# Attention as one staged pipeline that also projects its gates, and eight output-gate tiles computed beside the rwkv inputs

## The reference

```python
def attention_mixer(u_lat, u_ctx, ...):       # 8 query heads, 2 key/value heads, head size 128
    q, k, v, z = jnp.split(u @ w_in, ...)
    q = rms_norm(q, q_norm_g); k = rms_norm(k, k_norm_g)      # per head
    ql = apply_axial_rope(ql, ...); kl = apply_axial_rope(kl, ...)
    y = softmax(ql @ concat(kc, kl).T * d ** -0.5) @ concat(vc, vl)
    return (y * silu(z)) @ w_out
...
    p = rmsnorm(x, norm1_w) @ w_in
    z, xbc, dt_raw, p_rwkv, p_hgrn, p_gate = jnp.split(p, in_splits, axis=-1)
    y_ssm = ssd_branch(...)   @ w_branch_ssm      # ends with rmsnorm(y, ssm_norm_w)
    y_rwkv = rwkv7_branch(p_rwkv, ...) @ w_branch_rwkv
    y_hgrn = hgrn2_branch(p_hgrn, ...) @ w_branch_hgrn
    gates = jax.nn.sigmoid(p_gate).reshape(b, L, 3, 1024)
    mixed = gates[:, :, 0] * y_ssm + gates[:, :, 1] * y_rwkv + gates[:, :, 2] * y_hgrn
    x = x + mixed @ w_out
```

## Time and profile before

| | us |
|---|---|
| median of 3 runs | 2381.48 |
| lowest and highest run | 2377.84, 2381.9 |
| profiled execution, its own time | 2380.35 |
| its span in the trace | 2378.6 |

### The profile page before, as it was taken

The page is one execution under the profiler, slowest core; times in us unless marked ns, Lnnn a source line. Parts: engine busy times, 40 slices in busy tenths (PEclk is TensorE's granted clock), DMA queues, the critical chain, the costliest instruction groups (busy, mean ns, idle before and its releaser), DMA issues. The chain is left out here.

```text
span 2378.6 us, 40862 instructions
## 1 busy us (share of the span) xinstructions
PE 2021.5 (85%) x16732; PEld 1484.7 (62%) x16732; DVE 1059.6 (45%) x2136; ACT 577.9 (24%) x1248; POOL 76.0 (3%) x51
## 2 busy tenths in 40 slices
PE   5889898998989898896955687867989999879997
PEld 2356666565666656345633576644776798768886
DVE  4345756656575665102134318776445433211101
ACT  2033443434344343002012103222332321000000
POOL 0000110101010010000000000000000000000000
PEclk9889998999999998897967888986999999989998
DMA  8610101011010100212300132111012222324443
GB/s 332 266 54 2 55 1 56 1 55 55 2 55 1 55 1 2 106 71 76 107 0 0 71 118 107 71 66 41 29 55 94 82 101 85 110 106 156 162 159 124
DMA packets 50339, 183.72 MB, mean 77 GB/s; under 512 B 5744, under 2 KB 7152, under 8 KB 49648
## 3 DMA queue, kind: packets, MB, share of 16 engines
q1 hardware_dynamic: 50160, 181.18, 20.6%
HBM read 180.11 MB, written 1.05 MB: 76 GB/s over the span
## 5 line engine op out<-in xcount | busy, mean ns | idle before, releaser
L826 PE MATMUL banks<-u,w_ring 128*128 128x512 f32 x768 | 357.0, 602 | 6.6 <-PEq L195 6.6
L406 PE MATMUL banks<-u,w_ring 128*128 128x256 f32 x1088 | 248.4, 390 | 13.5 <-PEq L195 13.5
L406 PEld LDWEIGHTS banks<-u,w_ring 128*128 128x128 f32 x1088 | 212.4, 197 | 47.2 <-issue 17.8
L826 PEld LDWEIGHTS banks<-u,w_ring 128*128 128x128 f32 x768 | 141.7, 193 | 137.6 <-issue 134.5
L485 PE MATMUL banks<-u,w_ring 128*128 128x256 f32 (+1 forms) x640 | 158.7, 412 | 17.2 <-PEq L195 17.2
L485 PEld LDWEIGHTS banks<-u,w_ring 128*128 128x128 f32 x640 | 125.7, 197 | 49.9 <-issue 33.6
L485 PE MATMUL banks<-gated,w_ring 128*128 128x512 f32 (+1 forms) x384 | 141.0, 530 | 3.0 <-PEq L195 3.0
L485 PEld LDWEIGHTS banks<-gated,w_ring 128*128 128x128 f32 x384 | 74.0, 193 | 69.6 <-issue 66.3
L424 ACT ACTIVATE sq<-h 128x256 f32<-128x256 f32 (+1 forms) x40 | 14.5, 444 | 349.7 <-PEq L195 349.7
L853 DVE SCALAR_TENSOR_TENSOR acc<-raw,hc,acc 128x512 f32<-128x512 f32 x128 | 96.2, 752 | 4.6
L382 PE MATMUL banks<-u,w_ring 128*128 128x256 f32 x384 | 88.2, 380 | 0.0
(11 more groups left out here) (468 smaller groups left out, 3248.8 us busy)
## 6 DMA issues: line engine op xcount, KB each, us to landing
w_ring<-in_w SPq DMA_DIRECT2D x323, 512.0 KB, 6.0
h<-in_h SPq DMA_DIRECT2D x2, 2048.0 KB, 9.5
const_base<-in_const SPq DMA_DIRECT2D x1, 1216.0 KB, 5.4
const_part<-in_const SPq DMA_DIRECT2D x1, 1024.0 KB, 4.9
out<-u SPq DMA_DIRECT2D x1, 1024.0 KB, 4.8
const_part<-in_const SPq DMA_DIRECT2D x1, 640.0 KB, 4.4
const_part<-in_const SPq DMA_DIRECT2D x1, 512.0 KB, 3.5
w_rows<-in_rows SPq DMA_DIRECT2D x1, 512.0 KB, 5.7
```

The source lines that it names most:

```text
L406: last = nc.tensor.matmul(out, lhs[k], rhs[k], start=(k == 0), stop=(k == n - 1))
L826: mm = nc.tensor.matmul(self.places[m % len(self.places)][:, :], st.slot(m)[:, P * k:P * k + P], u[:, k, :], start=(k == 0), stop=(k == KT ...
```

## The change

Five things change together.

1. Attention is one stage, `attention`. The keys' part and the four pairs of heads stand in one set of lists. The softmax of a pair, its transposes and its value products run beside the scores of the next pair and the normalisation of the one after.
2. The eight gate tiles of attention are no longer projected ahead. Their 64 products stand in the new stage, between its first steps. The weight stream is reordered to key and value, query, gate.
3. Two of 24 output-gate tiles take the place of the padding in `ssd_heads`, and six more (48 products) are projected in `rwkv_inputs`. Since their place (`early`, the latent half of `h`) is still needed, `h` is stored to DRAM (`hold`, 1 MB) after norm1 and loaded back after the first `gated_linear`.
4. The norm of `ys` and its barrier are gone as a stage; its squares, adds, root and scaling stand in `rwkv_inputs`. There the small loads are waited for by the engines that need them.
5. `hgrn_heads` has 16 gate tiles left, four products in each level.

```diff
+def attention(nc, st, bank, C, pqz, pkv, qg, kg, rope, kf, v_t, gated, src):
...
+    extra = BesideGroups(nc, st, src, pqz[:, ATT_Q:2 * ATT_Q, :], ATT_Q, [bank[6][:, 0:SEQ], bank[5][:, 0:SEQ]], s, 0)
+    extra.per_group = 4
+    st.in_stage(ATT_Q // 4, 4, s["x_summed"], block)
...
+        def query_sums(i):
+            pe.wait_ge(s["q_sq"], i + 1)
+            pe.wait_ge(s["q_ready"], i)
+            column_sums(nc, C, bank[7], qsq[:, i % 2, :], 4).then_inc(s["sums"], 1)
...
+        def scores(i, n):
+            if n == 0:
+                pe.wait_ge(s["q_ready"], i + 1)
+            if i == 0 and n == 0:
+                pe.wait_ge(s["k_ready"], ATT_KV)
+            if i:
+                pe.wait_ge(s["exped"], 4 * i + n - 3)
+            nc.tensor.matmul(bank[n][:, :], tile(q_of(i), n), kf[:, i // 2, :], start=True, stop=True).then_inc(s["scores"], 1)
+        def turn(i, n):
+            at = 4 * i + n
+            pe.wait_ge(s["probs"], at + 1)
+            if at >= 2:
+                pe.wait_ge(s["turned_out"], at - 1)
+            else:
+                pe.wait_ge(s["x_out"], ATT_Q)
+            for t in range(TT):
+                mm = nc.tensor.transpose(tile(bank[4 + n % 2], t), tile(pr[:, i % 2, n, :], t), C("ident"))
+            mm.then_inc(s["turned"], 1)
+        def outs(i, j):
+            pe.wait_ge(s["turned_out"], 4 * i + 2 * j + 2)
+            if i and j == 0:
+                pe.wait_ge(s["gated"], i)
+            accumulate(nc, bank[6][:, SEQ * j:SEQ * j + SEQ], [v_t[:, i // 2, t, :] for t in range(TT)],
+                       [pt[:, j, t, :] for t in range(TT)]).then_inc(s["out"], 1)
...
+        extra.products(pe, 4)
+        pe.wait_ge(s["k_sq"], ATT_KV)
+        column_sums(nc, C, bank[7], ksq, ATT_KV * TT)
+        pe.wait_ge(s["q_sq"], 1)
+        column_sums(nc, C, bank[7][:, ATT_KV * TT:], qsq[:, 0, :], 4).then_inc(s["sums"], 1)
+        pe.wait_ge(s["v_out"], ATT_KV)
+        extra.products(pe, 12)
+        pe.wait_ge(s["root"], 1)
+        for h in range(ATT_KV + 1):
+            spread(nc, C, bank[h], rc[:, TT * h:TT * h + TT], TT).then_inc(s["spread"], 1)
+        extra.products(pe, 6)
+        for h in range(ATT_KV):
+            pe.wait_ge(s["k_norm"], h + 1)
+            nc.tensor.matmul(bank[3][:, SEQ * h:SEQ * h + SEQ], C("rot"), kf[:, h, CTX:TOK], start=True,
+                             stop=True).then_inc(s["k_rot"], 1)
+        query_turn(0)
+        query_sums(1)
+        extra.products(pe, 18)
+        query_roots(1)
+        for n in range(4):
+            scores(0, n)
+        extra.products(pe, 8)
+        query_turn(1)
+        extra.products(pe, 16)
+        for i in range(pairs):
             for n in range(4):
+                turn(i, n)
+                if i + 1 < pairs:
+                    scores(i + 1, n)
+                if i and n == 0:
+                    outs(i - 1, 1)
+                if i + 2 < pairs and n == 0:
+                    query_sums(i + 2)
+                if i + 2 < pairs and n == 1:
+                    query_roots(i + 2)
+                if i + 2 < pairs and n == 3:
+                    query_turn(i + 2)
+            outs(i, 0)
+        outs(pairs - 1, 1)
...
+        squared(1)
+        for c in range(5):
+            extra.copy_tile(act, link)
+        for n in range(4):
+            exped(0, n)
+            if n:
+                extra.copy_tile(act, link)
+        squared(2)
+        for i in range(pairs):
             for n in range(4):
+                turned(i, n)
+                if i + 1 < pairs:
+                    exped(i + 1, n)
+                if n == 2:
+                    gate(i)
+                if i + 3 < pairs and n == 3:
+                    squared(i + 3)
...
+        for i in range(pairs):
             for n in range(4):
+                if i + 1 < pairs:
+                    negmax(i + 1, n)
+                at = 4 * i + n + 2
+                if at < 4 * pairs:
+                    probs(at // 4, at % 4)
+                if i + 2 < pairs and n == 0:
+                    mean(i + 2)
+                if i + 2 < pairs and n == 2:
+                    scaled(i + 2)
+                if i + 2 < pairs and n == 3:
+                    roped(i + 2)
+                if i and n == 1:
+                    finished(i - 1)
+        finished(pairs - 1)
...
+def rwkv_inputs(nc, st, bank, C, src, ys, norm_cols, early, spilled, loaded, p, ps, tmp, mu0, mu1, w_up, g_up, a_up, vecs, w0_rows, lw, g_t, aa, kk, rc, bonus):
...
+        extra = BesideGroups(nc, st, src, early[:, 2:8, :], 6, [bank[b][:, 0:SEQ] for b in (6, 7, 6, 7, 4, 5)], s, 0, half_tanh=True)
+        extra.per_group = 6
+        st.in_stage(1, 6, s["x_summed"], block)
...
+            extra.products(pe, 2 * KT)
+            pe.wait_ge(*loaded)
...
-            pe.wait_ge(s["gd"], 1)
-            for t in range(ST):
-                nc.tensor.matmul(bank[6 + t][:, :], ps[:, 13, P * t:P * t + P], g_up[:, :], start=True, stop=True).then_inc(s["g_raw"], 1)
+            pe.wait_ge(s["x_out"], 1)
+            extra.products(pe, KT)
...
+            pe.wait_ge(s["x_out"], 3)
+            pe.wait_ge(s["n_added"], KT - 1)
+            column_sums(nc, C, bank[6], sq[:, 0, :], ST).then_inc(s["n_summed"], 1)
+            extra.products(pe, KT)
+            pe.wait_ge(s["a_in"], 4)
+            extra.products(pe, KT)
...
+            pe.wait_ge(s["n_root"], 1)
+            spread(nc, C, bank[6], roots, ST).then_inc(s["n_spread"], 1)
+            pe.wait_ge(s["gd"], 1)
+            for t in range(ST):
+                pe.wait_ge(s["x_out"], 4 + t)
+                nc.tensor.matmul(bank[(7, 4)[t]][:, :], ps[:, 13, P * t:P * t + P], g_up[:, :], start=True,
+                                 stop=True).then_inc(s["g_raw"], 1)
+            extra.products(pe, KT)
...
+            act.wait_ge(spilled, 16)
+            extra.copy_tile(act, link)
+            extra.copy_tile(act, link)
+            link(nc.scalar.activation(early[:, 0:2, :], p[:, n:n + 2, :], ACT.Tanh, scale=0.5))
+            for k_in in range(KT):
+                nc.scalar.activation(sq[:, k_in, :], ys[:, k_in, :], ACT.Square).then_inc(s["n_squared"], 1)
+            act.wait_ge(s["kk_raw"], 1)
+            link(nc.scalar.activation(tmp[:, 0:4, :], kk, ACT.Square), s["kk_sq"])
...
+            for k_in in range(1, KT):
+                dve.wait_ge(s["n_squared"], k_in + 1)
+                link(nc.vector.tensor_tensor(sq[:, 0, :], sq[:, 0, :], sq[:, k_in, :], ALU.add), s["n_added"])
+            dve.wait_ge(s["kk_sum"], 1)
+            link(nc.vector.tensor_scalar(rc[:, 0:16], bank[0][:, 0:16], 1e-12, None, ALU.add), s["mean"])
...
+            dve.wait_ge(s["n_summed"], 1)
+            link(nc.vector.tensor_scalar(roots, bank[6][:, 0:ST], 1.0 / D, EPS, ALU.mult, ALU.add), s["n_mean"])
...
+            dve.wait_ge(s["n_spread"], 1)
+            for k_in in range(KT):
+                link(nc.vector.scalar_tensor_tensor(ys[:, k_in, :], ys[:, k_in, :], norm_cols[:, k_in:k_in + 1], bank[6][:, 0:SEQ],
+                                                    ALU.mult, ALU.mult))
...
-                project(nc, st, bank, 4, 4, lambda k: u[:, k, CTX:TOK], SEQ, pqz)
                 project(nc, st, bank, 1, 4, lambda k: u[:, k, :], TOK, pkv)
+                project(nc, st, bank, 2, 4, lambda k: u[:, k, CTX:TOK], SEQ, pqz)
                 finish_loads(nc, loads, small)
-                with ExitStack() as e3:
-                    sq = sb("sq1", [P, 2 * TOK], e3)
-                    rs = sb("rs1", [P, TOK], e3)
-                    attention_keys(nc, bank, C, pkv, cc("kg"), rope, kf, v_t, sq, rs)
-                attention_heads(nc, bank, C, pqz, cc("qg"), rope, kf, v_t, gated)
+                attention(nc, st, bank, C, pqz, pkv, cc("qg"), cc("kg"), rope, kf, v_t, gated, lambda k: u[:, k, CTX:TOK])
...
+        hold = nc.dram_tensor("hold", (P, KT, SEQ), F32).ap()
+        early = h[:, :, CTX:TOK]
+        start_loads(nc, [(hold, early)], late)
...
-                norm(u, u, cc("ssm_norm_w"), 0)
-                finish_loads(nc, loads, small)
-                rwkv_inputs(nc, bank, C2, p_rw, ps, tmp, cc("rwkv_mu", 0, 14), cc("rwkv_mu", 14, 28), up[0:64], g_up, a_up,
+                rwkv_inputs(nc, st, bank, C2, latent, u[:, :, 0:SEQ], cc("ssm_norm_w"), early, late, (small, loads), p_rw, ps, tmp, cc("rwkv_mu", 0, 14), cc("rwkv_mu", 14, 28), up[0:64], g_up, a_up,
...
-                hgrn_heads(nc, st, bank, banks, C2, cs, p_hg, lf, kf, cc("hgrn_norm_w"), yh, work, latent, gates, 24, 6)
+                hgrn_heads(nc, st, bank, banks, C2, cs, p_hg, lf, kf, cc("hgrn_norm_w"), yh, work, latent, gates[:, 8:24, :], 16, 4)
...
-                gated_linear(nc, st, bank, count, 4, src, tiles, gates[:, 8 * b:8 * b + 8, :])
+                own = gates[:, 8 * b:8 * b + 8, :]
+                gated_linear(nc, st, bank, count, 4, src, tiles, own if b else early, own)
+                if b == 0:
```

(19 more changed lines are left out.)

261 lines of the change are left out of this document (127 added, 134 removed).

## The result

The changed kernel takes 2294.22 us (median of 4 runs, 2291.12 to 2297.01), the kernel before 2381.38 in the same session; the ratio is 0.9637, interval 0.9620 to 0.9653. That is 87 us less; the forecast was 2288 and 94 less.

A forecast was written before the change was run, and what follows sets the result against it. TensorE alone bounds hgrn; in attention no engine is full and work goes from hand to hand. From 2380.35 us, -27.6 - 32 - 27 - 8 + 0.5 = -94.1 gives 2286.2, stated as 2288; range 2276 to 2300, 8 in 10 2273 to 2308.

The forecast's parts named there:

- Projection, -27.6: Projection ahead of attention: 8 of 16 tiles of 256 leave it at 3.45 us each, 27.6 us less.
- Attention's stage, 92 forecast: Merged attention stage: 78 us of TensorE work plus 13 of waits, end at 92 against 124, 32 less.
- the detour of the roots: Attention loop: root of the pair after next goes over VectorE and GpSimd; 2 us in each of two pairs, 1 in third.
- The bounds of 79 and 141: Attention stage: 79 us with no wait at all, 141 with no overlap of pairs.
- hgrn, -27: hgrn stage: two of six products leave each of 32 levels, level 4.38 to 3.52 us; 27 less, bounds 22 and 28.
- Norm and rwkv inputs, -8: Norm merged into rwkv inputs: end at 1631.7 against 1639.9, 8 us less; bounds 12 less and 0.
- Store and load of `h`, +0.5: 1 MB store ahead of the weights at 1367 and its load back: 0.5 us more, bounds 0 and 4.
- Rival 1: Attention loop's steps lock together: a pair takes 15.3 us, loop 12 to 20 longer, total 2300 to 2308; chance 0.14.
- Rival 2: The rwkv merge gives nothing, as products sit ahead of what VectorE waits for: total 2296; chance 0.07.
- Rival 3: Clock stays low in the attention loop, 36 us of TensorE work double at worst: +35, total 2323; chance 0.06.
- the 2322: Total in us if the attention loop ran at about 1.2 GHz by the skill's clock rule.
- Rival 4: Fuller TensorE is given 1.2 GHz; in hgrn 127 us become 254, total 2415, slower than before; chance 0.02.

The follow-up runs named there:

- the second time: The changed kernel run again, unchanged, on the last experiment's chip: 2293.82 us (5 runs, 2291.68 to 2294.90).
- experiment 5: Changed kernel with all sixteen gate tiles projected ahead again and no gate products in attention, pairs still overlapped: 2304.41 us, 0.9684 of the kernel before.
- Experiment 7: Changed kernel with one of eight products of each gate tile in the rwkv inputs and hgrn stages, waits, copies and loads kept: 2246.33 us, 0.9439.
- six other executions: The changed kernel's second run and five experiments' runs with the same rwkv inputs lists, one without the wait for the store; that stage with its gap: 49.6 to 49.8 us.
- Experiments 3 and 10: 3: changed kernel, rwkv inputs' barrier before the small loads, 2293.52 us. 10: barrier, small loads, then weights, plus two attention reorderings, 2285.04 us.
- experiment 8: Changed kernel without the store of half of `h` to HBM, its reload and the waits for them: 2294.69 us, 0.9638 of the kernel before.
- after: The changed kernel itself, with all five parts of the change: 2294.22 us, 0.9637 of the kernel before.
- experiment 4: Changed kernel with ten of attention's eighteen gate products moved behind the second pair's query sums, eight left ahead: 2289.40 us, 0.9614 of the kernel before.

## Why the prediction held, and where it was off

- **Projection, -27.6:** measured to 0.1 us. The price of a tile (3.45 us) came from a stage that TensorE filled before and after.
- **Attention's stage, 92 forecast:** 95.3 and, the second time, 93.7. Its waits, put at 13, are 13.6 (TensorE is busy for 81.7 of the 95.3), but in other places. The uncovered wait for the second pair's sums was 3.56 (forecast 3.4). The five us that I gave to the detour of the roots were one wait of 0.97; in its place TensorE waits for the scaled and rotated query (1.24, 2.26 and twice 0.52). What was mis-sized is the work, 81.7 for 78: the sum was at full clock, and the stage's first half was granted 0.93. Twelve products from 1168.66 and eighteen from 1185.94 took 6.9 and 9.4 us, where 0.432 each gives 5.2 and 7.8; that is 3.3 of the 3.7. The bounds of 79 and 141 were needlessly wide, but experiment 5 shows the order of things: the merge with its overlap 47 us, filling about 10.
- **hgrn, -27:** -29.1. The level came out to 0.01 us. The 0.6 I held back for the heads' borders did not appear, and the stage's start ran warmer (3.9 us from its first matmul to the first level's sums, 4.8 before), as did its end by 0.3; neither was forecast. Experiment 7 says why it was safe: TensorE stays the bound there with seven eighths of its products gone, so little else could come late.
- **Norm and rwkv inputs, -8:** -4.2, and -2.7 to -2.9 in six other executions: the step that failed. Two terms were wrong. The wait for the norm's spread, put at 3, was 4.56, and 5.8 to 6.0 in the six others: the sixteen products ahead of it were reckoned at full clock (6.9 us) and took 8.5 and 9.8 to 10.0. So the stage proper is 44.3 us from the barrier, and 45.6 to 45.8 in the others, 7.5 to 6.0 less than 51.8 and not 8. What I left out altogether is the opening: the five loads are now issued in front of the barrier, and each engine stands 4.0 us for SyncE, where 0.7 lay between the stages before. I had counted a moved step's instructions on the compute engines and not its loads on SyncE's queue. Experiments 3 and 10 show that this is the queue and not the data: with the barrier issued first the gap is 1.2 us, and the 2.8 us reach the stage's end.
- **Store and load of `h`, +0.5:** nothing in the stages beside them (experiment 8).
- **Rival 1** (steps lock): the first three pairs began their transposes 11.8 and 14.4 us apart (1211.22, 1222.99, 1237.43), not 15.3, and the difference of the two is a values product (1.7), which the first interval doesn't hold, and longer waits for the query, less the wait for the root. **Rival 2** (the merge gives nothing): gave 6.0 to 7.5 inside the stage. **Rival 3** (clock low in the loop): 1.00 in the loop. My reading of busy share against clock was wrong both ways: the loop, busy for 81%, had 1.00 where I put 0.93, and the first half, busy for 43.64 of 48 us, had 0.93 where I put full clock. The Trainium skill (TensorE: Matmul & The Clock Gate, the section on a second failure mode of the clock) says that short idling between groups of matmuls can make the clock swing between its two levels. Here waits of 0.40 to 2.26 us left it at 1.00 in the loop of after, and only single steps ran slowly in experiment 4 (last section), so the trace does not bear it out as a price of this loop. The page says swing and not stay low, so the 2322 that I drew from it was the most that it could cost. **Rival 4** (1.2 GHz in hgrn): 0.99.

## What to carry to other kernels

Overlap first, filling second: moving products out of a full stage is worth their full price only as far as they fall into waits, and a thinned run of either stage shows how far. Put a product in front of each instruction that waits for a long chain on another engine. And when a stage's opening is moved, read the queue that issues its barrier: what stands ahead of it there is paid by every engine. Then look at which engine ends the stage: a wait of 3.87 us on another one cost nothing here.

## What the runs showed of the hardware

- Unused matmuls made the serial stage 12 us shorter: the granted clock rose from 0.72 to 0.94 in the first pair and from 0.75 to 1.00 in the second, and nothing else had changed (experiment 6).
- The same wait can leave the steps behind it at full speed or not: behind 2.26 us the rotation and the outputs took 1.13 and 1.89 us in after, and in experiment 4, with the same steps around them, half as much again or more. The granted clock of these few us was 1.00 in after and 0.65 to 0.79 there; no run shows why:

```profile
1227.88 1.92 PE L1393 MATMUL banks<-pqz,const_first 128*128 128x512 f32 x2 [2.26 <-DVE pqz L1532]
1229.60 2.83 PE L406 MATMUL banks<-att_pt,v_t 128*128 128x256 f32 x8
```

- Profiled executions of kernels that differ only behind a stage began it up to 12 us apart (1101.58 to 1113.88; the same program twice, 1103.08 and 1103.73). Whether the run or the edit behind it moves this point is open. Either way single spans can't carry a difference of 3 us, and five runs barely do.
- A barrier that stands in SyncE's queue behind five issued loads held all engines for 4.0 us; the issues took 2.7 of them (1532.08 to 1534.78).
